# Mixture-of-experts weights: the down matrices fetched by GpSimd on a queue of its own, with other slots, and the first group's gate/up placed ahead of the item table

## The reference

```python
logits = (tok @ w_router + b_router).astype(jnp.float32)
top_val, top_idx = lax.top_k(logits, TOP_K)          # 4 of 32 experts
top_w = jax.nn.softmax(top_val, axis=-1)
...
hgu = tok[rows] @ w_gu[e] + b_gu[e]                   # w_gu: (32, 1024, 2048)
gate = jnp.minimum(hgu[:, 0::2], SWIGLU_LIMIT)
up = jnp.clip(hgu[:, 1::2], -SWIGLU_LIMIT, SWIGLU_LIMIT)
act = (up + 1.0) * (gate * jax.nn.sigmoid(SWIGLU_ALPHA * gate))
y = act @ w_down[e] + b_down[e]                       # w_down: (32, 1024, 1024)
out = out.at[row_tok].add(y * wts[:, None])
```

## Time and profile before

| | |
|---|---|
| median of 3 runs | 1273.61 us (1273.03 to 1277.87) |
| the profiled execution's own time | 1270.95 us |
| its span on the core | 1269.1 us |
| PE busy | 1126.6 us (89%) |
| DVE, ACT, POOL busy | 306.2, 202.5, 17.4 us |
| bytes moved | 455.64 MB, mean 359 GB/s |
| of these by queue q1 (SyncE) | 454.55 MB |
| by q0 (GpSimd, software) | 0.13 MB |

### The profile page before, as it was taken

How to read it: one execution, slowest core, us unless ns; L and a number is a source line. 1 busy time by engine, 2 the same in 40 slices (tenths; PEclk the granted TensorE clock), 3 DMA queues, 4 the chain that set the end, 5 groups by cost and what they waited for, 6 DMA issues and landing times.

```text
span 1269.1 us, 19152 instructions
## 1 busy us (share of the span) xinstructions
PE 1126.6 (89%) x7479; PEld 520.7 (41%) x7480; DVE 306.2 (24%) x802; ACT 202.5 (16%) x441; POOL 17.4 (1%) x24
## 2 busy tenths in 40 slices
PE   9999999999999997759976947899798959799786
PEld 5665768888453332203322312233232313233221
DVE  2434443562142221102211201122121202122211
ACT  2116432353111110001110100011010101011100
POOL 0100000000000000000000000000000000000000
PEclk9999999999989998979988979899799989999998
DMA  9933437525689999999999999999999999999997
GB/s 323 348 134 132 131 134 265 177 94 218 253 345 375 427 427 429 429 426 430 427 427 428 429 427 429 429 417 429 429 428 428 427 427 428 429 429 428 428 428 311
DMA packets 58871, 455.64 MB, mean 359 GB/s; under 512 B 7636, under 2 KB 13624, under 8 KB 34136
## 3 DMA queue, kind: packets, MB, share of 16 engines
q1 hardware_dynamic: 58472, 454.55, 86.8%
q10 hardware_dynamic: 304, 0.53, 0.1%
q0 software_dynamic: 64, 0.13, 0.0%
HBM read 454.15 MB, written 1.05 MB: 359 GB/s over the span
## 4 chain that ended last, share of the span: by engine, by line
PE 63%; DMA 29%; SPq 6%; issue 1%; DVE 1%; ACT 0%; ACTq 0%; DVEq 0%
DMA mem<-in_w_gu 29%; PE bank L1027 17%; PE bank L1183 8%; PE bank L617 6%; PE bank L765 6%; PE bank L999 4%; SPq L400 4%; PE bank L1134 3%; PE bank L927 2%; PE bank L673 2%; PE bank L1006 2%; PE bank L961 2%; PE bank L606 1%; SPq L529 1%; PE bank L643 1%; PE bank L949 1%
## 5 line engine op out<-in xcount | busy, mean ns | idle before, releaser
L1027 PE MATMUL bank<-mem 128*32 128x512 f32 x2928 | 379.1, 649 | 134.7 <-DMA mem<-in_w_gu 132.8
L1027 PEld LDWEIGHTS bank<-mem 128*32 128x32 f32 x2928 | 89.8, 115 | 387.1 <-issue 200.4
L1183 PE MATMUL bank<-mem 128*32 128x512 f32 x1456 | 170.5, 597 | 0.0
L1952 DVE TENSOR_SCALAR mem<-bank 128x256 f32<-128x256 f32 x46 | 19.5, 425 | 471.1 <-PE bank L1027 471.1
L1495 ACT ACTIVATE mq<-bank 64x512 f32<-64x512 f32 x46 | 27.2, 591 | 527.5 <-PE bank L1183 524.2
L999 PEld LDWEIGHTS bank<-mem,sc 128*128 128x128 f32 x784 | 89.5, 192 | 20.2 <-issue 20.1
L999 PE MATMUL bank<-mem,sc 128*128 128x64 f32 (+1 forms) x784 | 92.9, 277 | 0.0
L1183 PEld LDWEIGHTS bank<-mem 128*32 128x32 f32 x1456 | 42.3, 110 | 120.2 <-issue 118.5
L617 PE MATMUL bank<-mem 128*128 128x512 f32 x192 | 83.5, 592 | 0.0
L1134 PE MATMUL bank<-mq,mem 128*128 128x512 f32 x176 | 80.3, 599 | 0.0
L765 PE MATMUL bank<-mem 128*128 128x256 f32 x320 | 71.6, 381 | 0.0
(11 more groups left out here) (316 smaller groups left out, 764.6 us busy)
## 6 DMA issues: line engine op xcount, KB each, us to landing
mem<-in_w_gu SPq DMA_DIRECT2D x128, 2048.0 KB, 40.1
mem<-in_w_down SPq DMA_DIRECT2D x63, 2048.0 KB, 38.8
mem<-in_w_in SPq DMA_DIRECT2D x13, 2048.0 KB, 11.7
mem<-in_w_out SPq DMA_DIRECT2D x2, 2048.0 KB, 8.5
mem<-in_w_mem_kv SPq DMA_DIRECT2D x4, 512.0 KB, 5.6
mem<-in_w_mem_kv SPq DMA_DIRECT2D x1, 2048.0 KB, 8.8
mem<-in_cmp_w_k SPq DMA_DIRECT2D x1, 2048.0 KB, 8.5
mem<-in_cmp_w_v SPq DMA_DIRECT2D x1, 2048.0 KB, 9.5
```

What stands on the lines that cost most here:

```text
L1027: mm = nc.tensor.matmul(BH[n][32 * s:32 * s + 32, :], xgT[:, k, 32 * n:32 * n + 32], w[:, c, 512 * s:512 * s + 512], start=k == 0, stop=k ...
L1183: mm = nc.tensor.matmul(BG[64 * hh + 32 * two:64 * hh + 32 * two + 32, :], actT[:, o:o + 32], w[:, r, 512 * hh:512 * hh + 512], start=d == ...
```

## The change

The down chunks (q = 4, 5) are issued by GpSimd instead of SyncE, on their own semaphores. In the loop SyncE runs `load_up` and GpSimd `load_down`, each with its own waits, so that neither holds up the other; the last `load_down` also waits until gate/up chunks 2 and 3 of the last expert have landed. The slots are dealt out anew. The two numbers of a round are packed into one. The router's logits are computed transposed (8 matmuls over all 256 tokens, four at a time in the column groups, and two that add the four parts up). One of the four `keep_x1` goes behind "rank". All eight column blocks of the first left item are gathered by themselves, in two halves, and its four gate/up chunks run before the first pair, the third ahead of the item weights; the first full gather then covers both groups. The constant tables follow.

```diff
         def slot_no(q, odd):
-            return q if not odd else NSLOT + q if q < 4 else 6 + q
+            return ((0, 1, 3, 4, 2, 5), (8, 9, 10, 11, 6, 7))[odd][q]
+
+        down_full = {(d, odd): S(f"down_full{d}{odd}") for d in range(2) for odd in range(2)}
...
+            full = w_full[n_slot] if q < 4 else down_full[q - 4, bool(odd)]
+            sp.dma_start(slot[n_slot].rearrange("p (c n) -> p c n", c=n), src).then_inc(full, 16)
...
-            arrived(sp, "hv")
-            load_chunk(sp, 1, 0, True)
-            for q in (5, 0, 1):
-                arrived(sp, ("bgn01", "bgn11", None, None, None, "pl11")[q])
+            for q in (0, 1):
+                arrived(sp, f"bgn{q}1")
                 load_chunk(sp, 0, q, False)
             arrived(sp, "nv3")
-            load_chunk(sp, 1, 1, True)
-            load_chunk(sp, 1, 4, True)
+            load_chunk(sp, 1, 2, True)
             arrived(sp, "pn11")
-            load_chunk(sp, 0, 2, False)
...
             sp.wait_ge(S("merged"), 8)
-            load_chunk(sp, 1, 2, True)
-            for q in (3, 4):
-                arrived(sp, f"wo{q - 3}1")
+            load_chunk(sp, 1, 0, True)
+            for q in (2, 3):
+                arrived(sp, f"wo{q - 2}1")
                 load_chunk(sp, 0, q, False)
-            arrived(sp, "lg")
-            load_chunk(sp, 1, 5, True)
...
+            arrived(sp, "lT")
+            load_chunk(sp, 1, 3, True)
             sp.wait_ge(S("x1_kept"), 1)
             sp.wait_ge(S("x2_ready"), 2)
-            load_chunk(sp, 1, 3, True)
+            load_chunk(sp, 1, 1, True)
+            def load_up(n, odd):
+                turn = sp.value_load(idx[0:1, bass.ds(n, 1)], min_val=0, max_val=NE * ITEMS - 1)
+                f, ahead = sp.snap(sp.to_reg(turn >> 5)), sp.snap(sp.to_reg(turn & 31))
                 for q in range(4):
                     sp.wait_ge(S("gu_done"), f * 4 + (q + 1))
                     load_chunk(sp, ahead, q, not odd)
...
+            arrived(pool, "hv")
+            load_chunk(pool, 1, 4, True)
             power(st[0:30, 119:120])
+            arrived(pool, "pl11")
+            load_chunk(pool, 0, 5, False)
+            arrived(pool, "nv3")
+            load_chunk(pool, 1, 5, True)
+            arrived(pool, "pn11")
+            load_chunk(pool, 0, 4, False)
...
+            def load_down(n, odd, final=False):
+                turn = pool.value_load(idx[0:1, bass.ds(n, 1)], min_val=0, max_val=NE * ITEMS - 1)
+                f, ahead = pool.snap(pool.to_reg(turn >> 5)), pool.snap(pool.to_reg(turn & 31))
+                for q in (4, 5):
+                    pool.wait_ge(S("down_done"), f * 2 + (q - 3))
+                    if final:
+                        pool.wait_ge(w_full[slot_no(q - 2, True)], 8 * NE)
...
+                        load_chunk(pool, ahead, q, not odd)
+            pool.wait_ge(S("order_ready"), 1)
+            with pool.Fori(0, NE // 2 - 2) as r:
+                load_down(r * 2 + 1, True)
+                load_down(r * 2 + 2, False)
+            load_down(NE - 3, True)
+            load_down(NE - 2, False, final=True)
...
+            b = begin("lT")
+            for k in range(KT):
+                g = k % 4
+                for i in range(NT):
+                    was_read(pe, f"xT{i}{k // 4}")
+                a = x1T[k // 2][:, k % 2, :] if k < 4 else x1T[2][:, k - 4, :]
+                mm = nc.tensor.matmul(b[32 * g:32 * g + 32, 0:SEQ], wr[:, k, :], a, start=k < 4, stop=k >= 4)
+            done(mm, "lT")
...
-            for i in range(NT):
-                for hh in range(2):
-                    mm = keep_x1(i, hh)
-            mm.then_inc(S("x1_kept"), 1)
+            for i, hh in ((0, 0), (0, 1), (1, 0)):
+                keep_x1(i, hh)
             pe.wait_ge(S("sel_ready"), 1)
             b = begin("rank")
...
+            keep_x1(1, 1).then_inc(S("x1_kept"), 1)
             b = begin("count")
...
+            left_gather(0)
+            pe.wait_ge(S("seats_ready"), 1)
+            b = begin("first")
+            nc.tensor.matmul(b[0:1, 96:96 + NE], C("seen")[0:NE, :], Hs, start=True, stop=True)
...
             pe.wait_ge(S("x_live"), 1)
-            first_up(w, 0)
...
-            first_up(w, 1).then_inc(S("gu_done"), 1)
+            up(0, 0, 0, 0)
             b = begin("rT")
...
+            left_gather(1)
             up(1, 0, 0, 0)
...
             done(mm, "it")
+            pe.wait_ge(S("x_live"), 2)
+            up(2, 0, 0, 0)
+            bias(0, 0)
             was_read(pe, "rT")
             pe.wait_ge(S("bdn_in"), 16 * 4)
             add_b_down()
-            pe.wait_ge(S("order_ready"), 1)
...
             item_weights()
-            pe.wait_ge(S("G_ready"), 1)
+            up(3, 0, 0, 0)
             was_read(pe, "it")
-            for c in range(4):
-                mm = gather_part(BX, c, 32 * c, Gm[:, :, 1, :])
-            mm.then_inc(S("g_full"), 1)
+            gather(0)
             was_read(pe, "itw")
-            for c in range(4):
-                mm = gather_part(BG, 4 + c, 64 * c, Gm.rearrange("p i g n -> p i (g n)"))
-            mm.then_inc(S("g_full"), 1)
```

More of the change, by code:

```diff
@@ L109 @@
 NB = 8
-X1 = ["xT00", "xT10", "wo11", "xT01", "lg", "xT11"]
-TAIL = ["rank", "count", "first", "rT", "it", "itw"]
+X1 = ["xT00", "xT10", "wo11", "xT01", "xT11"]
+TAIL = ["lT", "lg", "rank", "count", "first", "rT", "it", "itw"]
 BANK, TURN = {}, {}
@@ L119 @@
     else:
-        BANK[name] = {"xT00": 5, "xT10": 6, "xT01": 7, "xT11": 4, "lg": 6, "rank": 5, "count": 7,
+        BANK[name] = {"xT00": 5, "xT10": 6, "xT01": 7, "xT11": 4, "lT": 5, "lg": 6, "rank": 5, "count": 7,
                       "first": 7, "rT": 7, "it": 5, "itw": 4}[name]
@@ L530, in load_round @@
                                      b_gu[bass.ds(ahead, 1), :].rearrange("o (s n) -> (o s) n", s=4)).then_inc(brow_in[not odd], 16)
[L531 to L539, removed]
             sp.wait_ge(S("order_ready"), 1)
             with sp.Fori(0, NE // 2 - 2) as r:
[L543 to L546, removed]
+                load_up(r * 2 + 1, True)
+                load_up(r * 2 + 2, False)
+            load_up(NE - 3, True)
+            load_up(NE - 2, False)
             for i in range(NT):
@@ L579, in _ @@
                 power(st[:, c:c + 1], "nhalf")
+            def load_down(n, odd, final=False):
[5 more added lines that the diff above has]
+                        pool.wait_ge(w_full[slot_no(q - 2, True)], 8 * NE)
+                    if q == 5 and final:
+                        for h, sem in ((0, down_full[1, True]), (1, S("last_half"))):
+                            o = SLOT // 2 * h
+                            src = w_dn[ahead].rearrange("(p r) n -> p (r n)", p=P)[:, SLOT + o:SLOT + o + SLOT // 2]
+                            pool.dma_start(slot[SLOT_ODD_LAST][:, o:o + SLOT // 2], src).then_inc(sem, 16)
+                    else:
+                        load_chunk(pool, ahead, q, not odd)
[5 more added lines that the diff above has]
+            load_down(NE - 2, False, final=True)
         @block.tensor
@@ L974, in _ @@
             x1_turn(0, 1)
+            x1_turn(1, 1)
             pe.wait_ge(S("wr_in"), 16)
[L976 to L990, removed]
+            b = begin("lT")
[6 more added lines that the diff above has]
+            done(mm, "lT")
+            was_read(pe, "lT")
+            pe.wait_ge(S("late_in"), 32)
+            b = begin("lg")
+            for i in range(NT):
+                mm = nc.tensor.matmul(b[:, NE * i:NE * i + NE], lTs[:, P * i:P * i + P], C("sum32"), start=True, stop=True)
+            done(mm, "lg")
             for name in ("pn00", "pn01", "pn10", "pn11", "wo00", "wo01", "wo10", "wo11"):
@@ L1030, in up @@
                 mm.then_inc(S("gu_done"), 1)
-            def first_up(w, c):
-                for s in range(4):
-                    mm = nc.tensor.matmul(BH[0][32 * s:32 * s + 32, :], xgT[:, c, 0:32], w[:, c, 512 * s:512 * s + 512],
-                                          start=c == 0, stop=False, skip_group_check=True)
-                return mm
             def keep_x1(i, hh):
@@ L1225, in pair @@
                     either(before, lambda odd: down(0, before, odd))
-                pe.wait_ge(S("x_live"), j * 2 + 2)
-                third_up(left, 0)
-                if not first:
+                    pe.wait_ge(S("x_live"), j * 2 + 2)
+                    third_up(left, 0)
                     either(before, lambda odd: down(1, before, odd))
-                either(left, lambda odd: up(3, left, 0, odd))
+                    either(left, lambda odd: up(3, left, 0, odd))
                 if first:
@@ L1983, in _ @@
             dve.wait_ge(S("g_full"), 1)
-            gathered(xgT[:, 0:4, 32:64], BX[:, 0:128], gcol[:, 0:4], S("x_right"))
-            dve.wait_ge(S("g_full"), 2)
-            gathered(xgT[:, 4:8, :], BG[:, 0:256], gcol[:, 4:8], S("x_live"))
```

(2 more changed lines are left out.)

74 lines of the change are left out of this document (37 added, 37 removed).

## The result

| | before | after |
|---|---|---|
| median of 4 runs each | 1273.68 us | 1297.02 us (1295.27 to 1299.12) |
| ratio, 95% interval | | 1.0194 [1.0175, 1.0214] |
| profiled execution (span) | 1270.95 (1269.1) | 1299.12 (1297.5) |
| mean granted clock | 0.945 | 0.923 |

The change makes the kernel 23.3 us slower; the forecast was 1292, so 18.4 of it. The profiled execution of after is the slowest of its four and that of before lies under all of its four (1273.03 at the least), so the two traces differ by 28.4 us of span.

The account below looks back on a forecast made before the run. From 410 us on the time was taken as bytes over the DMA rate of 428 GB/s. Terms of +19.6 and -1.0 gave +18.6 us: 1289.5 for the profiled execution, 1292 for the median, range 1270 to 1304.

Parts of the forecast that it names:

- Part 3: Down loads on their own queue: down chunks pass gate/up chunks, and the hole after 844 us grows by 19.6 us.
- SyncE issues no load for about 57 us: Sign of a right forecast: before the hole at about 845 to 865, SyncE's gap in requests is 57 us instead of 41.
- Four chunks: Down chunks already served when the long expert's last gate/up chunk is in, leaving 19.6 us of work instead of 39.2.
- Rival (d): Queues share unequally and only two chunks slip ahead: +9.8 - 1, 1282 us; chance 0.10.
- Part 2: Router and first group, before the first down: -2.6 us if the clock holds, +1.9 if it falls; -1 taken.
- The tail is the same in both kernels: Behind the stream, the last down chunk, scatter and output were taken as the same before and after.
- The added waits: Last down loads held behind gate/up chunks 2 and 3: a cost of 0 to 2 us, taken as 0.
- No second hole: Outside the one hole the rate stays within 426 to 430 GB/s, so nothing was counted elsewhere.
- GpSimd's start and the rate: GpSimd's later load start, up to 4 us before 402.63, and the software queue's rate, up to +32 us; both taken as 0.
- rival (c): The software queue is slower, on top of the forecast: +10 to +32 us, 1302 to 1324; chance 0.11.
- rival (b): Two deep rows keep engines fuller, 434 instead of 428 GB/s, nothing slips ahead: 1266.7 to 1260.9 us; chance 0.07.
- Rival (a): The second queue gets no turn ahead or its lead is used up before 808: 1271.0 to 1275.5 us; chance 0.17.

Follow-up runs that it names:

- Experiment 4: The changed kernel, each down load also waiting for gate/up chunk 0 (first) or 1 (second) of its own expert to land; 1292.46 us, ratio 1.0182.
- experiment 1: The changed kernel with all loads back in SyncE's row in the old order, slots, router and first group staying changed; 1273.92 us, ratio 1.002.
- experiment 7: The changed kernel with gate/up chunk 3 of the first item run between the two full gathers; 1289.92 us, ratio 1.0133.
- experiment 5: The changed kernel without the two waits that hold the last expert's down chunks behind its gate/up chunks 2 and 3; 1305.3 us, ratio 1.0275.
- experiment 2: The kernel before with only the down loads issued by GpSimd, own semaphores and the added last-round wait; 1293.74 us, ratio 1.0157.

## Why the prediction was right, point by point

- **What bounds it: right.** One stream at 428 GB/s, and a time that empty engines move; the exception is the tail behind the stream, which the prediction left as it was. The three places found account for 26.8 of 28.4 us.
- **Part 3, 19.6 us: right in mechanism, place and size.** 20.1 us measured in after (20.9 less the 0.8 of before), 19.1 with the queue alone (19.9 less 0.8), 17.5 at another seat. The shares are equal (50.8% to 49.3%) when both rows are deep, down chunks landed after 18.2 us ("some 20"), gate/up came 9.8 us apart. The Trainium skill, "DMA: Bandwidth & Descriptors", Queues, rings and completion order, says that an engine goes round the rows with work; by that rule the shares are equal, and the trace agrees.
- **"SyncE issues no load for about 57 us": short.** Between two of SyncE's requests lay 74.7 us (795.08 to 869.78), and 62.9 from GpSimd's last request to SyncE's next. The 41 with which the 57 was compared runs from a down request (803.2), which SyncE no longer makes. The last gate/up chunk came 24.0 us later than before (832.24 against 808.22), some 3 of which are the later start; 57 instead of 41 allows for 16.
- **Four chunks: right in the difference, each side 0.4 to 0.7 of a chunk too high.** From the last take to the hole there was work for 17.8 us, 3.6 chunks and not 4. In before it was 35.8 us, 7.3 chunks and not the 8 (39.2 us) of the prediction, which for a stretch of 36.4 us would have left no hole at all where 0.8 us was read. The two overcounts cancel nearly, which is luck. Experiment 4 tells the rule from chance: with two allowed ahead the engines had work for 26.9 us, and the hole was 9.7. Rival (d), two only, is what that kernel is, not the change.
- **Part 2, -1.0 us: wrong in sign; the start lost +3.2 in after's trace and +1.6 in that of experiment 1, whose time is 2.3 us above before.** The chosen value was the failing step, not the reason for its bounds: I had named that two gathers in a row could drop the clock, priced it at +1.9 in all and then took the other side. The clock fell there for 10 us. In after the cost passed even the upper bound of 1.9: the second gather (6.99 against 3.71) and the down behind it (5.24 against 3.57) lose 5.0 us, not 4.5; the chunk behind the left half was slow as well (3.39 against 1.85, but also 3.29 in experiment 7); and the engines ran empty (16 GB/s in 390 to 395) until the first down freed its slot and GpSimd asked at 395.32. Experiment 7, which gives the clock back, has its first down at 386.57, where the prediction had it (385 to 390); after had it at 391.06. There the start loses 2.4 us less than before, close to the -2.6 that the prediction gave for a clock that holds.
- **"The tail is the same in both kernels": wrong, +3.5 us.** After the last experts' gate/up chunks came late, TensorE had 34 us of work without a gap from 1255.82 to 1290, with 3.64 + 7.02 + 4.41 us of it against about 1.85 + 3.73 + 3.65 at the full clock (the granted clock was 0.50 over 1255 to 1265), 5.8 us more. Experiment 7 has the same two queues and no such fall at this gather, and its tail is 10.9 us, as in before (11.1). So the 3.5 go with the clock and not with the queue as such. Where the last expert's order of arrival is changed as well (experiments 4 and 5), the tail is 18 to 19 us.
- **The added waits, 0 to 2 us: wrong in sign against leaving them out.** Without them it is 8.3 us more (experiment 5). What they cost against before was not measured by itself.
- **"No second hole": right for the change, wrong for the queue by itself** (4.5 us at 610, experiment 2). The slack there was smaller than I read from the flat 426 to 430, which shows that there is some and not how much.
- **GpSimd's start and the rate, both 0: right.** With the queue alone 350 to 410 moved 362 GB/s against 363, so its start cost nothing there. Pieces of 16 KB ran at the plateau of 428 through both queues, so rival (c) and rival (b) fall; 434 over ten microseconds is scatter. Rival (a) falls with the equal shares. Its "one packet per engine" was misread besides: 56 packets are 3.5 per engine.

In the profiled execution the forecast was 9.6 us low (1289.5 against 1299.1). Of these the start is 4.2 (+3.2 instead of -1.0), the tail 3.5 and the hole 0.5. The 5 us by which the median is above the forecast can't be split like this, since only the slowest execution of after has a trace.

Open: why experiment 2 has the second hole and after hasn't; the 1.6 us not located; whether two hardware queues would do the same. All loads of the loop in one software row, which would separate "second" from "software", were planned as an experiment that gave no result.

## What to carry to other kernels

Here one row of loads already kept the engines full, and the second queue added no bandwidth: it only changed which bytes came first, and the chunks that slipped ahead of what the consumer wanted next were paid back as empty engines where the consumer was longest on one buffer set. In such a case compute, for the longest consumer stretch, how many chunks are still outstanding when it starts, before and after, and multiply the difference by the time of a chunk. Holding loads back by waits repaired that only in part (9.4 us of hole and 13.5 us of new waits); one row in the order of use repaired it (experiment 1). The last consumer needs its inputs in order too: without the two waits that kept them so it was 8.3 us more.

## What the runs showed of the hardware

- Two deep queues with pieces of 16 KB, one hardware and one software, shared the 16 engines equally by bytes and by time (2.16 MB and 50.8% against 2.10 MB and 49.3% in 10 us), and their sum was the rate of one (428 GB/s).
- An issue of a 2 MB load took GpSimd 0.53 to 0.60 us, SyncE 0.34.
- Two full gathers in a row (2 x 32 matmuls) ahead of a down went with a fall of the granted clock to 0.50, the 1.2 GHz level, over 385 to 390 us; with one gate/up chunk between them it stayed at the 2.4 GHz level (1.00 over 380 to 390 in experiment 7, and 3.71 us for the second gather instead of 6.99).
